# Attention steps of one token tile instead of two, in a six-layer fp32 transformer forward on one core

## The reference, cut to what matters

```python
mix = dsa_attention / dilated_attention / moba_attention   # by layer: 0 and 3, 1, 2
mo = memory_attention(heads(qm), mk, mv)                   # no mask
mixed = concatenate([mix, mo]) @ w_out[i]
x = layer_norm(ALPHA * x + mixed, ln1_g[i], ln1_b[i])
x = layer_norm(ALPHA * x + swiglu(x, w_gate_up[i], w_down[i]), ln2_g[i], ln2_b[i])
```

## Time and profile before

| | us |
|---|---|
| median of 3 runs (1952.08 to 1953.87) | 1952.76 |
| profiled execution | 1967.28 |
| its span, first to last instruction | 1965.3 |
| TensorE busy in it | 1886.9 |
| GpSimd busy | 1520.2 |
| ScalarE busy | 938.8 |
| VectorE busy | 828.6 |
| mean granted TensorE clock | 0.986 |

### The profile page before, as it was taken

One profiled execution on the slowest core, in us unless ns is written; L12 is line 12 of the kernel. 1 busy time (PEld: TensorE's weight loads), 2 busy tenths in 40 slices (PEclk: granted clock), 3 DMA queues, 4 the chain that ended last, 5 costly groups with the idle time before them and its releaser, 6 DMA issues.

```text
span 1965.3 us, 27351 instructions
## 1 busy us (share of the span) xinstructions
PE 1886.9 (96%) x9610; PEld 1543.3 (79%) x9610; DVE 828.6 (42%) x1913; ACT 938.8 (48%) x1473; POOL 1520.2 (77%) x1332
## 2 busy tenths in 40 slices
PE   6999999999999999999999999999899999999998
PEld 5777888777888877788787778877788877778876
DVE  7784110446211245411057731126736344556534
ACT  3455444354444346444434644444437644545742
POOL 6758989885897977697976789796677886767784
PEclk9999999999999999999999999999999999999999
DMA  8444656564666554465545456664545555554442
GB/s 267 124 145 142 202 150 235 172 193 117 197 191 210 156 174 158 151 187 184 202 130 157 153 171 189 198 204 126 167 147 147 171 168 172 163 164 143 143 164 97
DMA packets 184269, 330.54 MB, mean 168 GB/s; under 512 B 12188, under 2 KB 44488, under 8 KB 184136
## 3 DMA queue, kind: packets, MB, share of 16 engines
q1 hardware_dynamic: 176224, 323.21, 53.6%
q10 hardware_dynamic: 7912, 5.59, 0.9%
HBM read 325.35 MB, written 3.41 MB: 167 GB/s over the span
## 4 chain that ended last, share of the span: by engine, by line
PE 82%; DVE 8%; POOL 5%; DMA 2%; issue 2%; ACT 1%; ACTq 0%; DVEq 0%
PE acc L1391 24%; PE acc L1392 23%; PE acc L1398 21%; POOL w_lo L1171 5%; PE tps L1338 4%; PE acc L1413 3%; PE ops L1455 2%; PE acc L1394 2%; PE tps L1431 2%; DMA raw<-in_w_down 1%; DVE QT L1550 1%; PE ops L1350 1%; DVE U L1820 1%; PE acc L1362 1%; PE acc L1364 0%
## 5 line engine op out<-in xcount | busy, mean ns | idle before, releaser
L1171 POOL TENSOR_TENSOR w_lo<-raw,w_hi 128x512 fp32r<-128x512 f32 (+2 forms) x1244 | 1479.6, 1226 | 407.2 <-ACT w_hi L1199 406.3
L1199 ACT CAST w_hi<-raw 128x1024 fp32r<-128x1024 f32 (+2 forms) x624 | 615.4, 991 | 777.7 <-PE acc L1398 597.7
L1391 PE MATMUL acc<-w_hi,xT_hi 128*128 128x512 f32 (+1 forms) x1808 | 692.1, 386 | 13.1 <-issue 3.1
L1392 PE MATMUL acc<-w_lo,xT_hi 128*128 128x512 f32 (+1 forms) x1808 | 670.6, 374 | 0.0
L1398 PE MATMUL acc<-w_hi,xT_lo 128*128 128x512 f32 (+2 forms) x1744 | 508.3, 373 | 1.1 <-DVE xT_lo L1650 1.1
L1391 PEld LDWEIGHTS acc<-w_hi,xT_hi 128*128 128x128 f32 x1808 | 344.4, 190 | 87.7 <-issue 22.8
L1392 PEld LDWEIGHTS acc<-w_lo,xT_hi 128*128 128x128 f32 x1808 | 345.0, 191 | 52.8
L1398 PEld LDWEIGHTS acc<-w_hi,xT_lo 128*128 128x128 f32 x1744 | 319.9, 190 | 60.5 <-DVE xT_lo L1650 2.8
L1710 DVE TENSOR_TENSOR H<-G,acc 128x512 f32<-128x512 f32 (+1 forms) x48 | 30.9, 643 | 334.0 <-PE acc L1398 334.0
L1391 PE MATMUL acc<-w_hi,hT_hi 128*128 128x512 f32 x352 | 139.5, 396 | 5.1 <-POOL w_lo L1171 5.1
L1392 PE MATMUL acc<-w_lo,hT_hi 128*128 128x512 f32 x352 | 137.2, 390 | 0.0
(11 more groups left out here) (196 smaller groups left out, 2011.9 us busy)
## 6 DMA issues: line engine op xcount, KB each, us to landing
raw<-in_w_gate_up SPq DMA_DIRECT2D x160, 512.0 KB, 3.9
raw<-in_w_in SPq DMA_DIRECT2D x104, 512.0 KB, 3.7
raw<-in_w_down SPq DMA_DIRECT2D x88, 512.0 KB, 4.0
raw<-in_w_out SPq DMA_DIRECT2D x48, 512.0 KB, 3.7
raw<-in_w_in_a SPq DMA_DIRECT2D x32, 512.0 KB, 3.7
raw<-in_w_in_b SPq DMA_DIRECT2D x20, 512.0 KB, 3.9
raw<-in_w_mem_kv SPq DMA_DIRECT2D x16, 512.0 KB, 4.4
raw<-in_w_gate_up SPq DMA_DIRECT2D x32, 256.0 KB, 2.8
```

Of the source, the lines that this page charges most:

```text
L1171: ins = nc.gpsimd.tensor_tensor(w_lo[:, r, i, 0:ch.width], raw[:, r, i, 0:ch.width], w_hi[:, slot, i, 0:ch.width].bitcast(F32), ALU.subtract)
L1199: nc.scalar.copy(w_hi[:, u.u % SPLIT, 0:u.nk, 0:u.chunk.width], raw[:, u.u % RAW, 0:u.nk, 0:u.chunk.width]).then_inc(S["hi_ready"], 1)
L1391: nc.tensor.matmul(o, hi[:, tok], wh, start=first_k, stop=False)
L1392: ins = nc.tensor.matmul(o, hi[:, tok], wl, start=False, stop=False)
```

## The change

A step is now two heads (or three maps) of one token tile, and there are 108 steps. In a layer the memory steps of tile 0 and tile 1 come first, then all heads of tile 0, then all heads of tile 1. A step of tile 0 has one key tile, one of tile 1 two; full steps have two in both. A step has one `turn` of all its blocks and one `take_turn`, where a pair had two of each. Buffers of six steps are in use (`SETS = 6`), with the logits in places of 256, 512 or 768 columns. Query and key transposes are made for each tile apart. `top_k` is one chain for each tile, tile 0 in 4 pieces of two rounds, tile 1 in 8 pieces of one round. `sub_scale` is one for each tile. Banks, planner costs and priorities change with it. Behind a norm the lag is eight units. The first block's output product loses `closing`, so tile 0 is five units ahead there; the other closing chunks get priority 0.7 and 0.8.

```diff
     def attention(self, steps):
+            s.before2 = self.steps[-2] if s.s >= 2 else None
+            s.same_set = self.steps[-SETS] if s.s >= SETS else None
+            s.slot = s.s % SETS
...
-                                 room=("acc", s.banks or score_banks))
+                                 room=("acc", s.banks or ([(2, 3)] if s.apart_maps or size > 512 else [(2,), (3,)])))
...
+            blocks = s.turned * s.key_tiles
+            s.turn = self.task("PE", "turn", s, 110 * blocks, "t_ready", done, prio=0, room=("tps", [(0,), (1,)]))
+            s.take = self.task("DVE", "take_turn", s, 160 + 1.03 * P * blocks, "t_taken",
+                               [s.turn, b2.values if b2 is not None else None], prio=0)
...
     def open_chunk(...):
                     if n < self.normed + SPLIT:
-                        last = min(last, self.normed - 1)
+                        last = n - SPLIT
...
-                                    prio=1 + t, room=room)
+                                    prio=0.7 + 0.1 * t if closing else 1 + t, room=room)
...
-            mask = p.stage(2400, "top_k", [groups[-1].add], src=(0, 1))
-            for r in range(1, TOPK // 8):
-                mask = p.stage(1800 if r + 1 < TOPK // 8 else 2900, "top_k", [mask], src=(r, r + 1))
+            for t in range(T):
+                added = [gr.add for gr in groups if gr.t == t][-1]
+                pieces = 4 if t == 0 else 8
+                for r in range(0, TOPK // 8, TOPK // 8 // pieces):
...
-            out = lin(w["w_out"][l], 8, "mixed", spec[:1], banks=[[(0,)], [(1,)]], rows=MIXED)
-        out += lin(w["w_out"][l], 8, "mixed", spec[1:], hold=[[scored]] * T, banks=ANY, rows=MIXED, closing=True)
+        late = [(2,), (3,), (1,), (0,)]
+        out = lin(w["w_out"][l], 8, "mixed", spec[:1], hold=[[], [scored]], banks=[[(0,)], late], rows=MIXED)
+        out += lin(w["w_out"][l], 8, "mixed", spec[1:], hold=[opened, [scored]], banks=[[(0,), (1,)], late], rows=MIXED)
...
-        combined = [s.outputs for s in steps]
-        sub = p.task("DVE", "stage", Stage("sub_scale", combined), 3200, None, combined)
-        gated = [p.stage(1500, "sub_gate", [sub, gained[t]], t=t, src=da, dst=da) for t in range(T)]
+        for t in range(T):
+            combined = [s.outputs for s in steps if s.t == t]
+            sub = p.task("DVE", "stage", Stage("sub_scale", combined, t=t), 3000, None, combined)
+            gated.append(p.stage(1500, "sub_gate", [sub, gained[t]], t=t, src=da, dst=da))
...
             def do_scores(k):
-                for t in range(T):
-                    c = tile_cols(s, t)
-                    for m in range(s.maps):
-                        (qt, base, n), (kt, kbase, _) = s.q[m], s.k[m]
-                        ins = nc.tensor.matmul(acc[:, k.slot[m], c], QT[base:base + n, qt, P * t:P * t + P],
-                                               KT[kbase:kbase + n, kt, 0:c.stop - c.start],
+                for m in range(s.maps):
+                    (qt, base, n), (kt, kbase, _) = s.q[m], s.k[m]
+                    ins = nc.tensor.matmul(score_columns(s)[:, m], QT[base:base + n, qt, tokens(s)],
+                                           KT[kbase:kbase + n, kt, 0:s.width], start=True, stop=True)
...
             def do_values(k):
+                    for src, col, n, m, half, p0 in s.v:
+                        for kt in range(s.key_tiles):
+                            i = m * s.key_tiles + kt
+                            ins = nc.tensor.matmul(ops[p0:p0 + n, slot, P * half:P * half + P],
+                                                   rows(src)[:, kt, col:col + n], turned[:, P * i:P * i + P],
+                                                   start=kt == 0, stop=kt == s.key_tiles - 1)
```

More of the change, by code:

```diff
@@ L511, in attention @@
             s.combine = self.task("DVE", "combine", s, cost, "combined",
[L512 to L517, removed]
+                                  [s.probs, s.same_set.outputs if s.same_set is not None else None], prio=0)
@@ L521, in attention @@
[L521 to L527, removed]
@@ L552, in lin, with takes @@
         return [p.open_chunk(weight, k_tiles, acts, spec, **kw) for spec in specs]
-    def takes(chunks):
-        return [ch.take[t] for ch in chunks for t in range(T)]
+    def takes(chunks, tiles=range(T)):
+        return [ch.take[t] for ch in chunks for t in tiles]
     def norm_tiles(fn, gain, fed, source, chunks=None, keep=False, also=((), ()), scale=2300, apply=1600, acts="x"):
@@ L632, in plan, with takes_qm @@
         mask = None
+        def takes_qm(t):
+            return takes([last] if kind == 0 else vq[:1], [t])
         if kind == 0:
@@ L714, in plan @@
-        steps = [pair(6 + i, i, "MKV", MEMW + P * i, width=FULL, banks=[(2, 3), (0, 1)]) for i in range(2)] + steps
-        for s in steps:
-            if s.width != FULL:
-                s.fed = takes(vq)
-        for i in range(6 if kind != 1 else 0):
-            by_four = vq[:1] if kind == 0 else vq[-1:]
-            steps[2 + i].fed = takes(by_four if i < 4 else [c for c in vq if c not in by_four])
-        for s in steps:
-            if any(out[1] >= 4 for out in s.out):
-                s.clear = [x_used]
@@ L724, in plan @@
-        n = len(steps)
+        x_used = list(p.used["x"])
+        pairs_turned = [[[] for _ in range(3)] for _ in range(T)]
+        for t in range(T):
+            for i0, n, part in ((0, 2, 0), (2, 4, 1)):
+                for dst, col in (("QT", 0), ("KT", MIX)):
+                    first, stop = col + P * i0, col + P * (i0 + n)
+                    if kind == 1:
+                        fed = [chunks[c] for c in sorted({c // CHUNK for c in (first, stop - 1)})]
+                    else:
+                        fed = [halved[part][dst == "KT"]]
+                    done = p.tile_heads(src, list(range(first, stop, P)), P, dst, i0, t, takes(fed, [t]), clear_qk)
+                    for j in range(i0 // 2, (i0 + n) // 2):
+                        pairs_turned[t][j] += [b.take for b in done]
@@ L725, in plan @@
         if not l:
             steps[0].apart = [groups[-1].turn, lambdas]
-        def turned_for(i):
-            if i < 2 or kind == 1:
-                return mem_qk if i < 2 else qk
-            return qk[i - 2 - i % 2:i - i % 2]
-        p.attention(steps, {i: [b.take for b in turned_for(i)] for i in range(n)}, banks)
-        last_values, mem_values = steps[-1].values, steps[1].values
+        p.attention(steps)
+        last_values, mem_values = steps[-1].values, steps[3].values
+        opened = []
@@ L1969, in outputs @@
[L1969 to L1979 removed]
+                to = rows(s.heads_out)[:, s.t, s.out:s.out + P]
@@ new lines, in outputs @@
+            def outputs(s):
+                if not s.flipped:
+                    heads_out(s)
+                    return
+                slot = s.values.slot[0]
+                dve.wait_ge(S["out_hi"], s.out_hi.n)
+                for half, tile, p0, p1 in s.out:
+                    hi, lo = act_tile("mixed", tile)
+                    ins = v.tensor_tensor(lo[p0:p1, tokens(s)], ops[p0:p1, slot, P * half:P * half + P],
+                                          hi[p0:p1, tokens(s)].bitcast(F32), ALU.subtract)
+                ins.then_inc(S["out_taken"], 1)
```

487 lines of the change are left out of this document (230 added, 257 removed).

## The result

The changed kernel takes 1977.93 us in the median of four runs (1972.52 to 1986.35), the kernel before 1952.48 (1952.08 to 1953.87) beside it. The ratio is 1.0133 [1.0097, 1.0169]: 25 us slower. The forecast was 1973, within 1946 to 1990, and slower with 0.72.

A forecast was written before the change was run, and what follows sets the result against it. The prediction took TensorE, busy 96% of the span, as the bound. It summed 37 for visits, -3.5 and -13.5 for waits and 0 for the output product to +20 us on 1952.8: 1973 us, range 1946 to 1990.

The forecast's parts named there:

- Visits, forecast +37: Attention on TensorE: splitting all 54 steps pays each score and value visit's fixed part twice, +37 us.
- the full sum: Added score and value visits on TensorE, if each stands between products: 41.5 us.
- the bound of 20: Added visits on TensorE, if every one touched another and about half the cost were saved: 20 us.
- Waits in the attention, forecast -3.5 and -13.5: Half the waits go: -3.5 us in layers 0 and 3, -13.5 at the two differential attentions, low clock included.
- Lag and priorities at closings, forecast 0 with -3 to +3: Norms and closing chunks: earlier units no gain, order changes only among products needed anyway; 0, order bounds -3 to +3 us.
- idle time outside those stretches: TensorE outside the stretches examined: idle time falling by more than 10 us would show the prediction wrong.
- Output product, forecast 0 (-1 to +2.7 for each layer): Attention's output product, four layers: tile 0 five units ahead instead of seven costs 0, bounds -1 to +2.7 us each.
- the cover is those heads and five units: Behind the output product, tile 1's last heads and five units hide tile 0's norm: 0 us.
- forecast about 6: Layer 2, first scores to end of output product: about 6 us longer, from six pairs and two memory steps.
- The first rival: Attention: added visits mostly touch, costing 20 us or less, and most of 34 us waits go; 1939 us, chance 0.18.
- The rival of the uncovered norm behind the output product: Output product, four layers: tile 1's heads not in between, four times 2.7 us; 1984 us, chance 0.12.
- VectorE as the bound in layers 0 and 3: Layers 0 and 3: added VectorE work costs two times 6 us and waits stay; 1988 us, chance 0.10.

The follow-up runs named there:

- new trace of before: The kernel before, unchanged, executed and traced once more: 1954.05 us, ratio 1.0002, span 1950.6.
- together: The kernel before with the pairs' value matmuls cut by tile, both parts following each other without products between: 1954.12 us, ratio 1.001.
- apart: The kernel before with value matmuls cut by tile and, in 84 of 108 visits, half a products task ahead of each tile's part: 1994.51 us, 1.0216.
- neither line: The changed kernel with the lag behind a norm and the priorities of closing chunks set back as before: 1991.29 us.
- true prices: The changed kernel with planner prices of sub_scale and sub_gate raised from 3000 and 1500 to 7400 and 3100 ns: 1968.62 us, ratio 1.0082.

## Why the prediction was right, and which of its steps were wrong

The time was right to 5 us, the sign too, but the sum held by terms that cancelled, and that they did is luck: the visits cost 9 us less than forecast, the waits in the attention 21 more and the output product 7 more, and two planner lines that I had put at nothing gave 13 back. By the traces (span after less span of the new trace of before, 25.5 us):

- **Visits, forecast +37: about +28.** The price of one was right, 0.66 and 0.86 forecast, 0.636 and 0.837 measured, values as well. The step that failed is "I take 37, a tenth below the full sum, since products are there to stand between in nearly all of the attention". By matmul starts, scores take 10.8 us more, values 6.4, the products leading into them 3.5, and the first products behind them, whose 0.11 us is part of the price, 7 (136 such returns in place of 64). The planner, with twice the tasks to place, puts many of them next to each other: 108 visits were added, but only 73 runs of small work between products (269 to 342), and 73 at 0.37 to 0.41 us are 27 to 30 us. That is between the full sum of 41.5 and the bound of 20. That a visit costs by leaving the products and not by its columns, which the prediction worked out from rows, is shown by the pair together and apart.
- **Waits in the attention, forecast -3.5 and -13.5: about +4.** This is 38.6 us (neither line, by span) less 28 for the visits and 7 for the output product, so it holds the low clock too and is what remains, not a sum of rows. The interval between matmul starts beyond the usual one, summed over the trace where it is above 0.15 us, rises by 13.1 us from before to the kernel with neither line, 7 of them at the output products. The step that failed is "Of the two stretches' 18.3 us idle and 8.5 us of clock I take half, 13.5". The 6.27 us wait for the gated rows behind the first differential attention went, as forecast (0.39 us now), and so did the 2.24 us behind the second. But the same chain, paid twice, stopped TensorE for 4.28 us behind the heads of the first and for 4.46 us in the middle of those of the second. The prediction had named this as a danger and not priced it; the run with true prices shows that it is 7 to 9 us. The 3.5 us for layers 0 and 3 did not come either. In layer 3 TensorE waits for probabilities (PT) behind top_k 2.32 us, where the longest such wait there was 0.88 us; in the changed kernel:
```profile
1106.60 0.44 PE L1467 MATMUL ops<-PT,U 128*64 128x128 f32 x4 [2.32 <-DVE PT L1937]
```
- **Lag and priorities at closings, forecast 0 with -3 to +3: -13.** The priorities alone are -17 in the changed kernel, and the lag is not told from 0. The step that failed is "changes only among products that TensorE has to do anyway". It does the same products, but which of them come first decides when tile 1's norm starts, and thus whether TensorE waits for it and then runs at the lower clock. The waits of 3.78 us stood in the trace ahead of the prediction (ended at 1619.75 and 1936.15), and no stretch of the earlier trace rows took them in. At the four places the interval excess falls from 19.9 to 3.4 us. I had said I would be wrong if idle time outside those stretches fell by more than 10 us. In all it did not, so the sign could not warn of this: it is 43.8 us in the new trace of before and 43.4 in the changed kernel (52.9 in the first trace, 8.59 of it the wait at 45.05), since new waits took what the four places gave.
- **Output product, forecast 0 (-1 to +2.7 for each layer): about +7.** By the progress of the traces over these four stretches the changed kernel loses 2.2, 2.1, 1.3 and 1.8 us. The step that failed is "the cover is those heads and five units": with closing restored the idle time goes. The wait of 0.82 us for x_rows, in layers 2 and 3 before, is now in all four layers, and others follow it: 0.69 us in each layer, 0.61 in layer 0 and 1.23 in layer 3. The idle time was to stay within 1 us; it did in layer 2 (0.98 to 1.84) and not in the others (0.29 to 2.12, 0.29 to 1.75, 1.01 to 2.89). The low clock is no part of it in layer 0 (1.00 in both windows above).
- **Layer 2.** From product 2700 to the end of the attention the changed kernel loses 4.9 us, with neither line 5.4; forecast about 6. The feed-forward kept 0.218 us a matmul.

The sum is 28 + 4 + 7 - 13 = 26 us. The first rival (cheap visits, waits gone) was right that visits touch more than I took, but they cost 28 us and not 20, and the waits moved rather than went. The rival of the uncovered norm behind the output product came in part, 7 us in place of its 11. The rule of the Trainium skill, TensorEngine Tiling (Array Packing), Instruction Overhead, of about 60 cycles for a matmul, by which this cut costs nothing, agrees with the cut alone (the run together, 1.001) and leaves out what the visits apart cost. VectorE as the bound in layers 0 and 3 is not borne out as priced; VectorE did end new waits in both layers.

## What to carry to other kernels

Where one engine is the bound and its list is written out ahead, price a new order twice: the switches it adds (here 0.4 us for each time small matmuls leave a stream of large ones and stand alone), and the moment at which the last result of a stage is ready. An order "of the same work" is not free: ending a projection's products for both tiles before starting the ones behind the norm was the largest gain in this study, 1% of the time, and it came from a line I had put at nothing. Look over the whole trace for the idle time an ordering can reach, and give a planner the duration that the trace shows for a chain of small VectorE operations beside a busy GpSimd.

## What the runs showed of the hardware that I had not expected

Cutting a matmul of 256 columns into two of 128 cost 0.04 us a visit of twelve in place of eight. The waits of 2.31 and 0.77 us at the end of layer 1 cost some 5 us by the progress of the traces: besides the 3.1 us of waiting, the products behind them ran at the lower level, 0.39 to 0.43 us apart, and a granted clock of 0.86 over the 12 us is 1.7 us of full-speed work.
